# A first stage that takes its input by halves, turns it between the products, and builds its sines later

## The chip, the cores and the metric

The kernel runs on one core of a Trainium2 chip. A core has a matrix engine (TensorE, PE in the rows; PEld is its weight load), a vector engine (VectorE, DVE), a scalar engine (ScalarE, ACT), a general engine (GpSimd, POOL) and a queue engine (SyncE, SP), all with their own instruction streams, which meet at semaphores; transfers run on 16 DMA engines and are issued from the SP and ACT streams. The metric is the device time of one execution in microseconds, the median of several.

## The reference

Two layers of a block (an input projection, a pooling branch, a latent attention with rotary positions, a gated merge) and then a second block (differential attention, a recurrent branch, a mixture of experts) over 16 meta tokens and 512 tokens of width 1024. What matters here is the very beginning of layer 0:

```python
meta = jnp.broadcast_to(meta_tokens[None].astype(x.dtype), (B, N_META, D_MODEL))
h_res = jnp.concatenate([meta, x], axis=1)
...
h = rmsnorm(h_res, norm_gain[l])
proj = h @ w_in[l]
u_pool, z_pool, c_q, c_kv, k_rope, z_mla, g_pool, g_mla = jnp.split(proj, IN_SPLIT_POINTS, axis=-1)
```

and, inside the attention, `apply_rope`, which needs the cosine and sine of position times frequency.

## The kernel before

Activations are kept transposed: `hres` holds 8 chunks of 128 features by T = 528 tokens. The input arrives as rows of tokens (`xin`, 4 x 128 tokens by 1024 features), so TensorE turns it: chunk c is four 128x128 transposes into one PSUM accumulator, and a copy (VectorE, or ScalarE for c = 2, 5, 7) puts it into `hres`.

Products are done in fp32 precision from two parts. An "upper" part is a rounded copy (`h_upper`, `weights_upper`, on ScalarE: the gain is multiplied in there), a "lower" part is what the rounding lost (`h_lower`, `weights_lower`, on VectorE in this stage), and each product is upper x upper, upper x lower and lower x upper: 3 matmuls for each of 8 chunks and each of 2 halves of the tokens, 48 matmuls of 128x264 for 128 output features. The products of the projection come in the order c0 to c7 (the latents), u0 to u3 (the pooling input), rope. c0 and c1 are done together, chunk by chunk, by `first_products`, so that they can begin when chunk 0 is there; the others by `product_split`. Weights come by SP in granules of 256 columns: cq0 serves c0 and c1, cq1 serves c2 and c3, and so on. `weights_upper(c + 3)` stands behind the emptying of product c on ScalarE, since there are three places for upper weights.

The norm is applied late: `squares` on ScalarE fills 8 tiles, POOL adds them up, the product `ss_h` with a matrix of ones sums over the partitions, ScalarE takes the root (`root`, a Sqrt), VectorE the reciprocal (`inverse`), and the u products are scaled with it when they are emptied.

Before all this, VectorE works out the rotation angles from the positions (12 small instructions), and ScalarE takes the two sines. A table of gains and biases (`vrows`, `vrows2`) is turned by TensorE as well ("vecs", "vec2"), and so are the sines ("trig"); `turn_tables` on TensorE and `turned_tables` on VectorE do the last two, in layer 0 behind c2, with `ss_h` ahead of them. TensorE runs `keep_busy` matmuls (products with nothing that anyone reads) while the input arrives.

PSUM has four accumulators, taken in turn; TensorE waits for the reader of the one it takes again. All engines run in program order, which is the order of the code.

Of the kernel before, what the change touches and what calls it, by code (L numbers as in the profile page):

```python
# [16 lines left out]
I32 = mybir.dt.int32  # L17
# [5 lines left out]
P = 128  # L23
D = 1024
# [20 lines left out]
LV = 22  # L45
# [156 lines left out]
def program(nc, a, out, known=None, debug=None):  # L202
    n = Counts(known)
    mark, at, now = n.mark, n.at, n.now
    with ExitStack() as ctx:
# [70 lines left out]
        vrows2 = qkf[:, 5 * D + P:5 * D + 2 * P]  # L276

# [30 lines left out]
        X_BY_ACT = (2, 5, 7)  # L308

# [86 lines left out]
        x_loaded = sem("x_loaded")  # L396
# [260 lines left out]
        def _(sp):  # L657
            sp.dma_start(const[:, :], a["const"][:, 0:K_TIE]).then_inc(const_loaded, 16)

            sp.dma_start(krope[NOPE:QK, 0, META:T].bitcast(I32),  # L660
                         a["positions"].to_broadcast([ROPE, SEQ])).then_inc(const_loaded, 16)

            sp.wait_ge(pool_made, at(pool_made, "vrows"))
            for l in range(LAYERS):
                r = LV * l
                for name, r0, k, m in (("norm_gain", 0, DC, P), ("q_a_norm_gain", 8, QC, P),
                                       ("kv_a_norm_gain", 14, KC, P), ("pool_scale", 16, PG, P),
                                       ("q_norm_gain", 20, 1, QK), ("k_norm_gain", 21, 1, QK)):
                    sp.dma_start(vrows[r + r0:r + r0 + k, 0:m],
# [23 lines left out]
            load_first(0, 2)  # L693
# [10 lines left out]
            load_first(2, 4)  # L704
# [110 lines left out]
        def _(pe):  # L815
# [17 lines left out]

            def done(ins, label):
                ins.then_inc(psum_filled, 1)
                mark(psum_filled, label)
# [71 lines left out]
            dst = accumulator("vecs", dve_evacuated)  # L908
            keep_busy(dst[:, 1, :], 7, work[:, 0, 0:512])
            pe.wait_ge(const_loaded, 32)  # L910
            pe.wait_ge(gains_loaded, at(gains_loaded, "gains"))
            done(nc.tensor.transpose(dst[:, 0, 0:LAYERS * LV], vrows[0:LAYERS * LV, :],
                                     ident[0:LAYERS * LV, 0:LAYERS * LV]), "vecs")
            pe.wait_ge(x_loaded, 80)
            dst = accumulator("meta", dve_evacuated)
            for c in range(DC):
# [3 lines left out]
            for c in range(DC):  # L920
                dst = accumulator(("x", c), act_evacuated if c in X_BY_ACT else dve_evacuated)
# [3 lines left out]
            def turn_tables():  # L925

                pe.wait_ge(vec_loaded, at(vec_loaded, "vec2"))
# [12 lines left out]
            for n.layer in range(LAYERS):  # L940
# [603 lines left out]
        def _(act):  # L1544
# [4 lines left out]
            for i in range(4):  # L1549
                act.dma_start(xin[:, i, :], a["x"][0, i * P:(i + 1) * P, :]).then_inc(x_loaded, 16)  # L1550
            act.dma_start(metain[0:META, :], a["meta_tokens"]).then_inc(x_loaded, 16)
            act.wait_ge(dve_made, at(dve_made, "angles"))

            nc.scalar.activation(sinT, krope[NOPE:QK, 0, :], ACT.Sin).then_inc(act_made, 1)
            mark(act_made)
            nc.scalar.activation(cosT, krope[NOPE:QK, 1, :], ACT.Sin, scale=-1.0,
                                 bias=small[NOPE:QK, 0:1]).then_inc(act_made, 1)
            mark(act_made, "trig")
# [60 lines left out]
            act.wait_ge(dve_evacuated, at(dve_evacuated, "vecs"))  # L1619
# [1631 lines left out]
```

## Time and profile before

| | us |
|---|---|
| median of 3 runs | 1812.49 |
| lowest and highest run | 1810.97, 1815.47 |
| the profiled execution's own time | 1814.62 |
| its span in the trace | 1812.7 |
| TensorE busy | 1751.2 (97%) |
| VectorE busy | 1181.4 (65%) |
| ScalarE busy | 876.7 (48%) |
| GpSimd busy | 342.9 (19%) |
| mean granted TensorE clock | 0.987 of full |

The span is the time from the first to the last instruction in the trace; the execution's own time has 1.9 us around it. TensorE is busy in nearly the whole span, so what counts is where it waits or where its clock is low. A clock of 0.50 in a row is 1.2 GHz, 1.00 is 2.4 GHz.

### The profile page before, as it was taken

How to read it: one execution, taken by the hardware profiler on the slowest of the kernel's cores; microseconds unless marked ns; L12 is line 12 of the kernel's file. 1: busy time of each engine (PE TensorE's matmuls, PEld its weight loads, DVE VectorE, ACT ScalarE, POOL GpSimd, SP SyncE). 2: the span in 40 equal slices, each digit the busy share in tenths (PEclk: the TensorE clock that was granted, in tenths of full speed). 3: DMA queues.
4: the chain of work that ended last, by engine and by line, in shares of the span. 5: the costliest groups of instructions: out<-in, count | busy, mean ns of one | idle time of the engine just before them, and what ended most of it. 6: DMA issues, size and time to landing. Idle time of an engine off the chain costs nothing.

```text
span 1812.7 us, 25327 instructions
## 1 busy us (share of the span) xinstructions
PE 1751.2 (97%) x10148; PEld 1440.3 (79%) x10148; DVE 1181.4 (65%) x1700; ACT 876.7 (48%) x1411; POOL 342.9 (19%) x228
## 2 busy tenths in 40 slices
PE   8999999999999999999999999999999999999993
PEld 6998788999898677788999776765568868888882
DVE  5575644554456655555776598586774566889896
ACT  5425434334334544334344365556552356777771
POOL 3323222001242322001000276310010120000001
PEclk8999999999999999999999999999999989999997
DMA  6203111323311212323222110213243449999994
GB/s 190 77 24 99 48 48 54 110 71 116 96 60 59 66 45 71 101 93 98 94 93 77 64 48 24 69 48 95 68 151 117 143 172 375 403 404 403 403 376 174
DMA packets 156095, 241.31 MB, mean 133 GB/s; under 512 B 9593, under 2 KB 101018, under 8 KB 155978
## 3 DMA queue, kind: packets, MB, share of 16 engines
q1 hardware_dynamic: 148602, 212.88, 34.2%
q0 software_dynamic: 4464, 16.25, 2.4%
q10 hardware_dynamic: 2912, 10.55, 1.5%
q8 instruction: 82, 1.34, 0.3%
q14 instruction: 35, 0.29, 0.1%
HBM read 223.41 MB, written 16.25 MB: 132 GB/s over the span
## 4 chain that ended last, share of the span: by engine, by line
PE 51%; DVE 5%; ACT 4%; issue 1%; DMA 1%; POOL 0%; POOLq 0%; ACTq 0%; DVEq 0%
PE acc L1408 15%; PE acc L879 10%; PE acc L1123 9%; PE acc L1148 7%; PE acc L1212 2%; PE acc L1226 2%; PE acc L1243 1%; PE acc L1392 1%; PE acc L1234 1%; PE acc L1108 1%; DVE upad L2749 1%; DVE qk L2749 1%; ACT v L2007 1%; DMA qk<-y_rows,back_rows 0%; PE acc L1030 0%
## 5 line engine op out<-in xcount | busy, mean ns | idle before, releaser
L879 PE MATMUL acc<-h_split,ring_split 128*128 128x264 f32 (+1 forms) x864 | 269.4, 312 | 0.0
L879 PEld LDWEIGHTS acc<-h_split,ring_split 128*128 128x128 f32 x864 | 162.3, 188 | 9.7
L1148 PE MATMUL acc<-ring_split,h_split 128*128 128x256 f32 x384 | 107.9, 281 | 0.0
L879 PE MATMUL acc<-h_split,qk_split 128*128 128x264 f32 (+1 forms) x288 | 92.6, 322 | 1.3 <-DVE ring_split L2253 1.3
L879 PE MATMUL acc<-ring_split,qk_split 128*128 128x264 f32 (+1 forms) x288 | 92.2, 320 | 0.0
L2253 DVE TENSOR_TENSOR ring_split<-ring,o_split 128x1024 fp32r<-128x1024 f32 (+1 forms) x32 | 44.9, 1418 | 64.3 <-ACT o_split L1569 64.1
L3065 POOL TENSOR_TENSOR latent<-latent 128x528 f32<-128x528 f32 x18 | 26.8, 1490 | 292.9 <-ACT latent L1564 292.5
L2253 DVE TENSOR_TENSOR ring_split<-ring,qk_split 128x1024 fp32r<-128x1024 f32 (+1 forms) x56 | 59.4, 1070 | 34.0 <-ACT qk_split L1569 34.0
L879 PE MATMUL acc<-h_split,krope_split 128*128 128x264 f32 (+1 forms) x240 | 79.4, 331 | 1.9 <-POOL ring_split L3079 1.9
L879 PE MATMUL acc<-ring_split,krope_split 128*128 128x264 f32 (+1 forms) x240 | 77.0, 321 | 0.0
L3079 POOL TENSOR_TENSOR ring_split<-ring,krope_split 128x1024 fp32r<-128x1024 f32 x20 | 48.1, 2406 | 152.5 <-ACT krope_split L1569 152.5
L1123 PE MATMUL acc<-h_split,ring_split 128*128 128x512 f32 x192 | 75.6, 394 | 0.0
L1148 PEld LDWEIGHTS acc<-ring_split,h_split 128*128 128x128 f32 x384 | 72.3, 188 | 0.0
L1569 ACT ACTIVATE qk_split<-ring 128x1024 fp32r<-128x1024 f32 (+2 forms) x60 | 57.4, 965 | 23.4 <-PE acc L879 22.6
L2500 DVE TENSOR_SCALAR latent<-latent,small 128x144 f32<-128x144 f32 (+4 forms) x72 | 66.2, 919 | 2.6
L879 PE MATMUL acc<-work_split,qk_split 128*128 128x264 f32 (+1 forms) x192 | 61.6, 321 | 0.0
L879 PE MATMUL acc<-upad_split,ring_split 128*128 128x264 f32 (+1 forms) x192 | 61.6, 321 | 0.0
L879 PE MATMUL acc<-h_split,o_split 128*128 128x264 f32 (+2 forms) x208 | 61.4, 295 | 0.0
L879 PE MATMUL acc<-ring_split,o_split 128*128 128x264 f32 (+2 forms) x208 | 60.7, 292 | 0.0
L3197 POOL DMA_INDIRECT latent<-h_rows,rows_of x16 | 15.1, 943 | 237.3 <-PE acc L1392 219.6
L879 PEld LDWEIGHTS acc<-h_split,qk_split 128*128 128x128 f32 x288 | 54.1, 188 | 5.7 <-issue 1.7
L879 PEld LDWEIGHTS acc<-ring_split,qk_split 128*128 128x128 f32 x288 | 54.2, 188 | 4.1
(599 smaller groups left out, 5571.8 us busy)
## 6 DMA issues: line engine op xcount, KB each, us to landing
ring<-in_w_in SPq DMA_DIRECT2D x64, 1024.0 KB, 5.2
ring<-in_w_expert_gate SPq DMA_DIRECT2D x10, 2048.0 KB, 12.7
ring<-in_w_expert_up SPq DMA_DIRECT2D x10, 2048.0 KB, 12.0
ring<-in_w_expert_down SPq DMA_DIRECT2D x10, 2048.0 KB, 13.2
ring<-in_w_out SPq DMA_DIRECT2D x12, 1024.0 KB, 5.2
y_rows<-gate ACTq DMA_DIRECT2D x16, 512.0 KB, 6.9
hres<-in_w_expert_up SPq DMA_DIRECT2D x3, 2048.0 KB, 11.6
qk<-in_w_expert_down SPq DMA_DIRECT2D x3, 2048.0 KB, 14.4
```

The costliest lines, as they stand in the source:

```text
L879: ins = nc.tensor.matmul(dst[0:rows_, half, 0:x.shape[1]], w[:, k, :], x, start=(k == 0 and i == 0), stop=(k == last and i == 2), skip_gro ...
L1123: ins = nc.tensor.matmul(dst[:, 0, :], w[:, k, :], x, start=(k == 0 and i == 0), stop=(k == DC - 1 and i == 2), skip_group_check=True)
L1148: ins = nc.tensor.matmul(dst[:, side, 0:WIDE], x[k][:, rows_], w, start=(k == 0 and part == 0), stop=(k == DC - 1 and part == 2), skip_gro ...
L1212: ins = nc.tensor.matmul(lx_at[-1], w[:, k, :], moved[k], start=x == 0, stop=x == LX_PASSES - 1, skip_group_check=True)
L1226: ins = nc.tensor.matmul(dst[:, c, :], q2[r, hd, i * P:(i + 1) * P], k2[r, hd, :], start=True, stop=True)
L1408: ins = nc.tensor.matmul(dst, x, w, start=start and i == 0, stop=stop and i == 2, skip_group_check=True)
L1569: nc.scalar.activation(dst, src, ACT.Copy).then_inc(act_made, 1)
L2253: made(nc.vector.tensor_tensor(dst, src, up.bitcast(F32), ALU.subtract), label)
L2500: made(ts(probs[s % 3][0:nt, 0:t0 + nt], probs[s % 3][0:nt, 0:t0 + nt], r, None, ALU.mult), ("p", s))
L2749: made(nc.vector.tensor_tensor_scan(m_[:, back_], a_[:, back_], x_[:, back_], 0.0, ALU.mult, ALU.add), ("scan", u))
L3065: ins = nc.gpsimd.tensor_tensor(latent[:, 0, :] if c < DC - 1 else sum_sq, latent[:, 0, :], latent[:, c, :], ALU.add)
L3079: nc.gpsimd.tensor_tensor(dst, src, up.bitcast(F32), ALU.subtract).then_inc(pool_made, 1)
```

## The change

All of it is in the first stage of layer 0. The input comes in two halves of the features instead of four quarters of the tokens, in turn with the weights: cq0 from SP beside half 0 from ACT, cq1 only once half 1 has landed. The identity matrix and the first gain come by their own small transfers; the other constants, the positions and the gains come behind. Chunks 0 to 3 are turned ahead of the products (with short `keep_busy` matmuls between them), chunks 4 to 7 behind the products of k = 0 to 3, in the accumulators that chunks 2 to 5 had. On ScalarE each chunk's square stands behind its upper part, not behind all of them. The angles are worked out on VectorE between the lower weights of c3 to c7, the sines follow the emptying of c6, and `ss_h`, the tables and what reads them stand behind c7 in layer 0.

```diff
+        SUMS_AT = (7, 2)
+        ANGLES_AT = 6
...
-            load_first(0, 2)
+            load_first(0, 1)
+            sp.wait_ge(x_loaded[1], 16)
+            load_first(1, 2)
+            sp.dma_start(angles[:, 0, META:T].bitcast(I32),
+                         a["positions"].to_broadcast([ROPE, SEQ])).then_inc(const_loaded, 16)
+            sp.dma_start(const[:, P:], a["const"][:, P:K_TIE]).then_inc(const_loaded, 16)
+            load_first(2, 4)
...
+                    if n.layer == 0 and k < 4:
+                        n.layer = None
+                        turn_input(k + 4)
+                        n.layer = 0
...
-            keep_busy(dst[:, 1, :], 7, work[:, 0, 0:512])
+            keep_busy(dst[:, 1, :], 3, work[:, 0, 0:512])
...
+            def turn_input(c):
+
+                if c % 4 == 0:
+                    pe.wait_ge(x_loaded[c // 4], 16)
+                by = act_evacuated if c in X_BY_ACT else dve_evacuated
+                if c < 4:
+                    dst = accumulator(("x", c), by)
+                else:
+                    dst = accumulator_again(("x", c), by, 4 - c % 2)
                 for i in range(4):
                     ins = nc.tensor.transpose(dst[:, 0, i * P:(i + 1) * P], xin[:, i, c * P:(c + 1) * P], ident)
                 done(ins, ("x", c))
+
+            for c in range(4):
+                turn_input(c)
+                keep_busy(acc[:, 3, 1, 0:256], 1 if c < 2 else 0, work[:, 0, 0:256])
+            keep_busy(acc[:, 3, 1, :], 3, work[:, 0, 0:512])
...
                     product_split(("c", c), act_evacuated, h_up, h_low)
-                    if c == 2:
-                        product("ss_h", act_evacuated, [ones[:, :]], lambda k: sum_sq,
-                                before=lambda k: pe.wait_ge(square_sum, at(square_sum, "sum", back=1)))
+                    if c == SUMS_AT[n.layer]:
                         if n.layer == 0:
                             n.layer = None
                             turn_tables()
                             n.layer = 0
+                        product("ss_h", act_evacuated, [ones[:, :]], lambda k: sum_sq,
+                                before=lambda k: pe.wait_ge(square_sum, at(square_sum, "sum", back=1)))
...
+            input_upper(0)
+            input_copy(2)
+            input_upper(1)
+            first_upper(0)
+            first_upper(1)
+            for c in range(2):
+                squares(c, ("x", c), ("sq0", c))
+            for c in range(2, 4):
+                input_upper(c)
+                squares(c, ("x", c), ("sq0", c))
...
-                    if c == 2:
+                    if n.layer == 0 and c == ANGLES_AT:
+                        n.layer = None
+                        rotation_tables()
+                        n.layer = 0
+                    if c == SUMS_AT[n.layer]:
                         root("ss_h", inv[:, :], D, 1)
...
-                for i in range(3 if n.layer == 0 else 2, 6):
-                    weights_lower(JOBS_A, i)
-                inverse("ss_h", inv[:, :])
                 if n.layer == 0:
+                    for i in range(3, DC):
+                        weights_lower(JOBS_A, i)
+                        if i < 7:
+                            n.layer = None
+                            (angles_begun, angles_turns, angles_reduced, angles_ended)[i - 3]()
+                            n.layer = 0
                     n.layer = None
                     turned_tables()
                     n.layer = 0
-                for i in range(6, DC):
-                    weights_lower(JOBS_A, i)
+                    layer_vectors()
+                    inverse("ss_h", inv[:, :])
```

How the instructions stand now: first TensorE at the start of the program, up to the first product (`const,qk` are transposes of the input, `work,ones` is `keep_busy`, L895 and L915 are the first products). Before:

```order
L841 MATMUL acc<-work,ones 128x512 x6
L912 MATMUL acc<-const,qk 128x44 [waits gains_loaded,const_loaded]
L917 MATMUL acc<-const,qk 128x16 [waits x_loaded]
L917 MATMUL acc<-const,qk 128x16 x7
L923 MATMUL acc<-const,qk 128x128 x8
...
L895 MATMUL acc<-h_split,o_split 128x264 [waits dve_made,act_evacuated,dve_evacuated,pool_made]
```

and of the change:

```order
L940 MATMUL acc<-const,qk 128x16 [waits meta_loaded]
L940 MATMUL acc<-const,qk 128x16 x7
L954 MATMUL acc<-const,qk 128x128 [waits x_loaded0]
L954 MATMUL acc<-const,qk 128x128 x3
L861 MATMUL acc<-work,ones 128x256
L954 MATMUL acc<-const,qk 128x128 x4
L861 MATMUL acc<-work,ones 128x256
L954 MATMUL acc<-const,qk 128x128 [waits dve_evacuated]
...
L861 MATMUL acc<-work,ones 128x512 x3
L915 MATMUL acc<-h_split,o_split 128x264 [waits dve_made,dve_evacuated,pool_made]
```

Four chunks instead of eight stand ahead of the first product, and `keep_busy` has moved from ahead of the input to between and behind its chunks.

Then VectorE in layer 0, from the lower part of c7's weights to that of u2's (L2253 and L2344 are `weights_lower`; the one from `zp_split` behind the reciprocal of `inv` is u0's). Before, u0's stands behind c7's, both behind the reciprocal:

```order
L2324 RECIPROCAL inv<-inv 128x528 [waits act_evacuated]
L2288 COPY vec<-acc 128x121 [waits psum_filled,dve_step]
L2292 COPY trig<-acc 128x160 [waits psum_filled]
...
L2253 TENSOR_TENSOR ring_split<-ring,o_split 128x8x128 [waits act_made] x2
L2349 TENSOR_TENSOR trig<-trig,rope_gain 128x160 [waits rest_loaded]
L2350 TENSOR_TENSOR trig<-trig,rope_gain 128x160
L2253 TENSOR_TENSOR ring_split<-ring,zp_split 128x8x128 [waits act_made]
```

and of the change:

```order
L2344 TENSOR_TENSOR ring_split<-ring,o_split 128x8x128 [waits act_made]
L2402 COPY vecs<-acc 128x36 [waits psum_filled]
L2405 COPY vec<-acc 128x121 [waits psum_filled]
...
L2446 RECIPROCAL inv<-inv 128x528 [waits act_evacuated,dve_step]
L2480 TENSOR_TENSOR trig<-trig,rope_gain 128x160 [waits rest_loaded,dve_step]
L2481 TENSOR_TENSOR trig<-trig,rope_gain 128x160
L2344 TENSOR_TENSOR ring_split<-ring,zp_split 128x8x128 [waits act_made]
```

The reciprocal, which waits for ScalarE's root of `ss_h`, has moved from ahead of the lower weights of c6 and c7 to behind them, and u0's lower weights still stand behind it.

And TensorE between c7 and u0. Before, u0 (L879) follows c7 directly; of the change:

```order
L899 MATMUL acc<-h_split,ring_split 128x264
L967 MATMUL acc<-const,qk 128x44 [waits act_evacuated,gains_loaded,const_loaded]
L971 MATMUL acc<-const,qk 128x121 [waits act_evacuated,vec_loaded]
L977 MATMUL acc<-const,trig 16x32 [waits act_evacuated,act_made]
...
L880 MATMUL acc<-gate,ones 128x264 [waits square_sum,act_evacuated]
L880 MATMUL acc<-gate,ones 128x264
L899 MATMUL acc<-h_split,zp_split 128x264 [waits dve_made,dve_evacuated]
```

The tables and `ss_h` (L880) now stand between c7 and u0, and u0 is the next thing behind them.

## Rows read from the trace of the kernel before

**Rows 1.** A stretch of the head: length, busy time (and instructions) of each engine, clock, DMA.

```profile
20.00:22.00 2.00, 0.00 (x0) 0.00 (x0) 1.70 (x3) 1.99 (x3) 0.00 (x0) 0.50 1.10 344
```

**Rows 2.** Timeline of TensorE in the head: start, length, line, operation, count.

```profile
1.54 9.25 PE L841 MATMUL acc<-work,ones 128*128 128x512 f32 x14 [1.54 <-DVE work L2219]
...
6.79 0.33 PEld L841 LDWEIGHTS acc<-work,ones 128*128 128x128 f32 x1 [0.52 <-issue]
7.63 0.19 PEld L841 LDWEIGHTS acc<-work,ones 128*128 128x128 f32 x1 [0.50 <-issue]
...
11.58 2.84 PE L923 MATMUL acc<-const,qk 128*128 128x128 f32 x24
18.57 1.12 PE L923 MATMUL acc<-const,qk 128*128 128x128 f32 x4 [0.97 <-DVE hres L2275]
22.20 0.56 PE L895 MATMUL acc<-h_split,o_split 128*128 128x264 f32 x1 [2.51 <-DVE ring_split L2265]
...
28.20 0.28 PE L895 MATMUL acc<-h_split,o_split 128*128 128x264 f32 x1
```

**Rows 3.** DMA: GB/s in 40 slices of 1 us; the last quarter of the input.

```profile
GB/s 0 38 206 421 377 362 399 408 399 182 337 349 345 350 350 332 309 238 385 350 348 341 324 168 93 53 54 8 2 0 0 0 0 0 0 0 0 28 163 388
...
qk<-in_x ACTq DMA_DIRECT2D x1, 512.0 KB, 7.7
```

**Rows 4.** Groups by form, 0 to 26 us: busy us, mean ns, idle before.

```profile
L2265 DVE SCALAR_TENSOR_TENSOR ring_split<-hres,vecs,h_split 128x528 fp32r<-128x528 f32 x8 | 6.1, 765 | 1.3 <-ACT h_split L1616 1.3
L1616 ACT ACTIVATE h_split<-hres,vecs 128x528 fp32r<-128x528 f32 x8 | 5.9, 734 | 2.4 <-DVE hres L2275 2.3
...
L2275 DVE COPY hres<-acc 128x512 f32<-128x512 f32 x5 | 3.3, 686 | 0.3 <-PE acc L923 0.3
...
L2253 DVE TENSOR_TENSOR ring_split<-ring,o_split 128x1024 fp32r<-128x1024 f32 x2 | 2.4, 1224 | 0.1
...
L1569 ACT ACTIVATE o_split<-ring 128x1024 fp32r<-128x1024 f32 x2 | 2.1, 1041 | 0.0
...
L1625 ACT ACTIVATE hres<-acc 128x512 f32<-128x512 f32 x3 | 1.7, 575 | 0.0
```

**Rows 5.** Timeline of TensorE at the starts of c2, c3 and u0.

```profile
36.55 0.28 PE L879 MATMUL acc<-h_split,zp_split 128*128 128x264 f32 x1
...
44.11 0.39 PE L879 MATMUL acc<-h_split,o_split 128*128 128x264 f32 x1
...
73.22 0.28 PE L879 MATMUL acc<-h_split,zp_split 128*128 128x264 f32 x1
```

**Rows 6.** Timeline of ScalarE: the squares, the root behind c2, the emptying of c7.

```profile
25.30 4.36 ACT L1564 ACTIVATE latent<-hres 128x528 f32<-128x528 f32 x8
...
44.65 1.28 ACT L1644 ACT_TABLE_LOAD   x1
45.94 0.70 ACT L1644 ACTIVATE inv<-acc,small 128x528 f32<-128x528 f32 x1
...
73.42 0.61 ACT L1655 ACTIVATE work<-acc 128x528 f32<-128x528 f32 x1 [3.74 <-PE acc L879]
...
74.42 1.06 ACT L1569 ACTIVATE o_split<-ring 128x1024 fp32r<-128x1024 f32 x1
```

**Rows 7.** Timeline of VectorE: the reciprocal, the gain products, u0's lower weights.

```profile
46.67 3.45 DVE L2324 RECIPROCAL inv<-inv 128x528 f32<-128x528 f32 x1 [0.45 <-ACT inv L1644]
...
59.60 0.31 DVE L2349 TENSOR_TENSOR trig<-trig,rope_gain 128x160 f32<-128x160 f32 x1
...
63.91 1.58 DVE L2253 TENSOR_TENSOR ring_split<-ring,zp_split 128x1024 fp32r<-128x1024 f32 x1 [3.76 <-ACT zp_split L1569]
```

**Rows 8.** Stretches around an idle gap later on: length, TensorE busy (instructions), clock, DMA.

```profile
576.00:577.00 1.00, 0.00 (x0) 1.00 0.00 0
577.00:578.00 1.00, 0.15 (x1) 0.81 0.00 0
...
581.00:582.00 1.00, 1.00 (x6) 0.98 0.00 0
```

More of the change, by code:

```diff
@@ L276, in program @@
         vrows2 = qkf[:, 5 * D + P:5 * D + 2 * P]
+        first_gain = qkf[:, 5 * D + 2 * P:5 * D + 3 * P]
+        angles = v[:, :, :].rearrange("p c t -> p (c t)")[NOPE:QK, 0:2 * T].rearrange("p (a t) -> p a t", a=2)
         sum_sq = gate[:, 1, :]
@@ L395, in program @@
         const_loaded = sem("const_loaded")
-        x_loaded = sem("x_loaded")
+        x_loaded = [sem(f"x_loaded{i}") for i in range(2)]
+        meta_loaded = sem("meta_loaded")
+        ident_loaded = sem("ident_loaded")
+        first_gain_loaded = sem("first_gain_loaded")
         vec_loaded = sem("vec_loaded")
@@ L657, in _, with load_gains @@
         def _(sp):
[L658 to L664, printed above, removed]
+            def load_gains(l):
                 r = LV * l
@@ L832, in accumulator, with accumulator_again @@
                 return acc[:, slot, :, :]
+            def accumulator_again(label, reader, back):
+                for x in jobs[-back]:
+                    released(*x)
+                slot = (len(jobs) - back) % ACCS
+                jobs[-back] = [(label, reader, n.layer)]
+                n.slots[label, n.layer] = slot
+                return acc[:, slot, :, :]
             def done(ins, label):
@@ L2231, in _ @@
-            big = 1.5 * 2 ** 23
-            chain(ts(turns, ang, 1.0 / (2 * math.pi), big, ALU.mult, ALU.add))
-            chain(ts(turns, turns, -big, None, ALU.add))
-            rest, parts = 2 * math.pi, []
-            for bits in (8, 12, 24):
-                e = 2.0 ** (bits - 1 - math.floor(math.log2(abs(rest))))
-                parts.append(math.trunc(rest * e) / e if bits < 24 else rest)
-                rest -= parts[-1]
-            for part in parts:
-                chain(stt(out=ang, in0=turns, scalar=-part, in1=ang, op0=ALU.mult, op1=ALU.add))
@@ L2241, in _, with angles_begun @@
-            chain(ts(krope[NOPE:QK, 0, :], ang, 3.1415925, -3.1415925, ALU.min, ALU.max))
-            dve.wait_ge(dve_step, now(dve_step))
-            made(stt(out=krope[NOPE:QK, 1, :], in0=krope[NOPE:QK, 0, :], scalar=-1.0,
-                     in1=krope[NOPE:QK, 0, :], op0=ALU.mult, op1=ALU.max), "angles")
-            result("vecs")
-            slot = n.slot(("vecs"))
-            evacuated(nc.vector.tensor_copy(vecs[:, :], acc[:, slot, 0, 0:LAYERS * LV]), "vecs")
+            def angles_begun():
+                dve.wait_ge(const_loaded, 32)
+                nc.vector.tensor_copy(ang[:, 0:META], const[NOPE:QK, K_META:K_META + META])
+                chain(nc.vector.tensor_copy(ang[:, META:T], angles[:, 0, META:T].bitcast(I32)))
+                chain(ts(ang[:, META:T], ang[:, META:T], float(META), None, ALU.add))
+                chain(ts(ang, ang, const[NOPE:QK, K_FREQ:K_FREQ + 1], None, ALU.mult))
@@ new lines, in angles_turns, with angles_reduced @@
+            def angles_turns():
+                big = 1.5 * 2 ** 23
+                chain(ts(turns, ang, 1.0 / (2 * math.pi), big, ALU.mult, ALU.add))
+                chain(ts(turns, turns, -big, None, ALU.add))
+            def angles_reduced():
+                rest, parts = 2 * math.pi, []
+                for bits in (8, 12, 24):
+                    e = 2.0 ** (bits - 1 - math.floor(math.log2(abs(rest))))
+                    parts.append(math.trunc(rest * e) / e if bits < 24 else rest)
+                    rest -= parts[-1]
+                for part in parts:
+                    chain(stt(out=ang, in0=turns, scalar=-part, in1=ang, op0=ALU.mult, op1=ALU.add))
@@ new lines, in angles_ended @@
+            def angles_ended():
+                chain(ts(angles[:, 0, :], ang, 3.1415925, -3.1415925, ALU.min, ALU.max))
+                dve.wait_ge(dve_step, now(dve_step))
+                made(stt(out=angles[:, 1, :], in0=angles[:, 0, :], scalar=-1.0,
+                         in1=angles[:, 0, :], op0=ALU.mult, op1=ALU.max), "angles")
+            result("first_gain")
+            slot = n.slot(("first_gain"))
+            evacuated(nc.vector.tensor_copy(vecs[:, 0:DC], acc[:, slot, 0, 0:DC]), "first_gain")
@@ L2332, in _ @@
                     n.layer = 0
-                for i in range(6, DC):
-                    weights_lower(JOBS_A, i)
+                    layer_vectors()
+                    inverse("ss_h", inv[:, :])
+                else:
+                    for i in range(2, 6):
+                        weights_lower(JOBS_A, i)
+                    inverse("ss_h", inv[:, :])
+                    for i in range(6, DC):
+                        weights_lower(JOBS_A, i)
                 def gain_of(x, count):
```

146 lines of the change are left out of this document (92 added, 54 removed).

## The prediction

> **What bounds the kernel now.** The page first: TensorE is busy for 97% of the 1812.7 us. So a change here is worth the time by which it moves a product of TensorE that everything behind it follows, less any wait that it adds. Then the timeline of the head [rows 2]: keep-busy matmuls from 1.54 to 10.8 us, six chunks turned in 2.84 us from 11.58, the last one at 18.57, the first product at 22.20. Between 20 and 22 us TensorE does nothing and its clock is at 0.50, 1.2 GHz [rows 1]; ScalarE and VectorE are both busy there, so the wait is for the elementwise work of chunk after chunk. Third, the starts of the later products [rows 5]: c2 at 36.55, c3 at 44.11, u0 at 73.22, so c3 to c7 take 5.82 us each without a wait, and 44.11 - 36.55 - 5.82 = 1.74 us is `ss_h` with the tables. Last, what stands around the root of `ss_h`, on ScalarE and VectorE [rows 6, 7].
>
> **The change part by part.**
>
> *Transfers.* By the slices [rows 3] 2.21 MB had moved at 9 us. Half 0 (1.05 MB), cq0 (1.05 MB) and the small pieces (0.13 MB) make 2.23 MB, so half 0 has landed at 9.1 us at the latest if the two share evenly, and at 8.5 if it gets two thirds (0.43 MB of smalls and cq0 first, then 1.05 x 1.5). I take 8.8. Before, the whole input had landed at about 9.8 us (issued near 2.1, 7.7 to landing [rows 3]). Half 1 lands at about 12.3 (3.28 MB in the same slices) and cq1 at about 17, both ahead of their use. The angles need constants and positions only at some 35 us. The gains land behind; the tables need them at some 65 us. These cost nothing under cover of c2 to c7; without it a late one would be its own delay.
>
> *The head, to the first product.* It needs chunk 0 turned, emptied and split, and, in this order on ScalarE, upper 0, the copy of chunk 2, upper 1, then the upper weights of c0 and c1; then VectorE's two lower weights. Lengths [rows 4]: copy 0.69 (VectorE) and 0.58 (ScalarE), upper part 0.73, upper weights 1.04, lower weights 1.22. A turned chunk is 2.84/6 = 0.47 us at the high clock and 1.12 at the low one [rows 2]; a keep-busy matmul of 512 columns is two passes, 0.84 apart at the low clock (6.79 to 7.63) and half that behind it, so the 256-column one is 0.85 or 0.43.
> At the high clock from 8.8: chunk 2 is turned at 8.8 + 3 x 0.47 + 2 x 0.43 = 11.1; copy 11.7, upper 1 12.4, upper weights 13.5 and 14.5, lower weights of c1 16.0 with the semaphores between. At the low clock chunk 2 is turned at 8.8 + 3 x 1.12 + 2 x 0.85 = 13.9, and the same chain ends at 18.7. Three keep-busy matmuls end at 14.1 and, if the clock has risen by then, at 17.6: hidden; if it stays low they end at 20.1 and hold the products.
> Which clock? Before, weight loads shortened at 7.63, after 6.1 us of unbroken keep-busy work [rows 2]. Now that work ends at 1.54 + 6 x 0.85 = 6.65, some small transposes follow, then TensorE waits for half 0. So the high clock at 8.8 is not sure, and may come during the chunks. I take the middle, 17.3, and keep 16.0 and 18.7 as ends (20.1 as the far one).
>
> *The products c0 and c1.* 96 matmuls at 5.82/48 = 0.121 us are 11.6, and four chunks turned between them 4 x 0.47 = 1.9: 13.5 us, so c2 starts at 30.8 instead of 36.55, 5.75 earlier (before, 14.35 for the same 96, of which 5.8 at the low clock, 22.2 to 28.0 [rows 2]). ScalarE must keep up: from its upper weights at some 16 us, eight squares (4.4 [rows 6]), six uppers (4.4), two copies (1.2), one upper weights (1.0) are 11, with waits for chunks 5 and 7 about 12.5: 28.5, against 29.4 when the last chunk's products begin. Hidden, with 1 us to spare; each us beyond would be on the path. POOL's sum ends 1.4 us behind the last square; it then holds c0's emptying for nothing, since c3's weights have 5.8 us of c2 as cover.
>
> *The sines, angles, squares.* VectorE's 12 angle instructions lie between lower weights that have two products of 5.82 us as cover; the sines end 0.9 us before c7 does: 0.2 + 2.06 behind c6's end to the end of the upper weights, then a table load of 1.28 and two sines, taken as 0.70 each like the Sqrt [rows 6]. Cost nothing; without the cover up to 1 us at the "trig" transposes.
>
> *`ss_h` behind c7: the wait it adds.* Call U the time at which c7's matmuls have been issued (73.22 before, when u0 started at once). Now c2 to c7 take 6 x 5.82 = 34.9, so U = 30.8 + 34.9 = 65.7. TensorE's own work behind it is 1.74 + 0.23 ("vecs"), to U + 1.97. Then u0 needs its lower weights, and these stand on VectorE behind the reciprocal of `ss_h`. That chain [rows 6, 7]: ScalarE empties c7 from U + 0.20 (73.42), ends its upper weights at U + 2.26 (75.48), loads the Sqrt table (1.28) and takes the root, which by the rows 44.65 to 46.64 are 1.99: U + 4.25. The reciprocal, 3.45: U + 7.73. Two gain products, 0.24 apart and 0.31 long: U + 8.32. The lower weights, 1.58 beside a working POOL: U + 9.90. u0 starts at U + 9.95, 75.65. TensorE idles 8.0 us (7.6 if the subtraction takes the 1.22 of [rows 4]). Before, this chain had c3 to c5 as cover. Behind u0, in the same queue, wait u1's and u2's lower weights, which u0's own time covers.
> The row has 1.28 us for a table load, with the Sqrt 0.01 us behind it. The Trainium skill (ScalarE: Activation LUTs, "What ACT_TABLE_LOAD costs") gives 2.66 for a switch, 1.38 of it a drain; no such drain shows here; by it the wait would be 9.4 and the sum 1.4 higher.
>
> *The clock behind the wait.* Later in this trace TensorE idled from about 575.5 to 577.9, the clock fell before 578 and was back at 581: 3.2 us at half speed, 1.6 lost [rows 8]. In the head 5.8 us at half speed lost 2.75 (14.35 against 11.6). An idle time of 8 us will bring it down; the cost is 1.6 to 2.8, and I take 2.3, nearer the head's, which runs the same stream of matmuls.
>
> **The sum.** Head -5.75; `ss_h` and tables only moved; "vecs" +0.23; wait +8.0; clock +2.3: +4.8 us. The shift should go through unchanged, since transfers and engines behind it are released by TensorE's products. The span becomes 1817.5 and the profiled execution's 1814.62 about 1819.4; the median of the runs, 1812.49, becomes 1817.3.
>
> **The rivals.** Changes within 0.3% (5.4 us) are about what this kernel's measurement can't tell from none.
> *Slower by more: the low clock in the head.* The input's chunks are turned at 1.2 GHz, the first product begins at 18.7 to 20.1, c2 at 32.2 to 33.6: the sum is +6.2 to +7.6, 1818.7 to 1820.1. It decides from a first product at about 17.9. For it: keep-busy ends at 6.65 where the clock rose only at 7.63. Against: transposes go on in that time.
> *The input lands no earlier.* If half 0 with cq0 beside it lands at 9.8, as the whole did, the head is 1.0 later: +5.8, 1818.3. Against it: only 2.23 MB must move, not the 2.4 before.
> *A fast head.* High clock from 8.8, first product at 16.0, and 1.6 for the clock behind the wait: +2.8, 1815.3.
> *Faster.* If u0 did not feel the chain behind c7, wait and clock would go and the sum be 4.8 - 8.0 - 2.3 = -5.5, 1807. The order of instructions on VectorE speaks against it: no cover stands between c7 and u0.
>
> **How the numbers follow.** Forecast, +4.8 with the clock rising among the chunks: 0.36, of which 0.08 lies over the bound. Fast head 0.20. Low clock 0.22. Late input 0.14. Faster 0.08, 0.02 of it within the bound. So within 0.3%: 0.28 + 0.20 + 0.02 = 0.50; slower: 0.08 + 0.22 + 0.14 = 0.44; faster 0.06. The forecast's own range is 1815 to 1819; with the fast head and the low clock, and the runs' spread of some 2 us on both sides, 1812.5 to 1821.5 leaves out the fast case and the far ends.
>
> **What would show it.** A first product (first-products line) near 17.3, c2 near 30.8 and u0 near 75.7; in front of u0 an idle time of 8 us put down to VectorE's lower weights; the clock at 0.5 for some us behind it; the Sqrt table load directly behind c7's upper weights. It is wrong if u0 starts within 2 us of c7's end, if ScalarE falls behind in the products of c0 and c1 (waits on VectorE's lower parts there), or if later stages take up the shift.

## The result and the profile after

| | before | after |
|---|---|---|
| median of 11 runs, us | 1812.49 | 1818.94 |
| the profiled execution's own time, us | 1814.62 | 1819.18 |
| its span, us | 1812.7 | 1817.2 |
| mean granted TensorE clock | 0.987 | 0.986 |

One of the 11 runs after took 2482.72 us, at a mean clock of 0.651; it is left out of the ratio and hardly moves the median. The ratio is 1.0032, with a 95% interval of 1.0024 to 1.004: 5.8 us slower by the ratio (6.45 by the two medians). The interval has the bound of 0.3% inside, so the change is slower, but whether by more than the bound can't be told. The time lies 1.6 us above the forecast of 1817.3, within its range.

The timeline of TensorE in the head of the changed kernel (start, length, line, operation, count; in brackets the idle time before and what ended it) answers to [rows 2, 5]; L915 is `first_products`, L899 `product_split`:

```profile
1.54 4.38 PE L861 MATMUL acc<-work,ones 128*128 128x512 f32 x6 [1.54 <-DVE work L2298]
...
9.35 1.12 PE L954 MATMUL acc<-const,qk 128*128 128x128 f32 x4 [1.61 <-DMA qk<-in_x]
...
12.82 1.92 PE L954 MATMUL acc<-const,qk 128*128 128x128 f32 x8
...
17.49 0.36 PE L915 MATMUL acc<-h_split,o_split 128*128 128x264 f32 x1
...
27.78 0.39 PE L915 MATMUL acc<-h_split,o_split 128*128 128x264 f32 x1 [0.64 <-DVE ring_split L2356]
...
32.85 0.28 PE L899 MATMUL acc<-h_split,zp_split 128*128 128x264 f32 x1
```

Half 0 is there at 9.35; the first product starts at 17.49, 4.71 earlier than before. The clock is low while the chunks are turned (a stretch with its clock; the mean is 0.55 in the microsecond before it and 0.53 in the one behind it, so it fell at about 8.1 and rose at about 14.95), and VectorE's lower weights of c0 and c1 end at 17.34 and 18.48:

```profile
9.00:14.00 5.00, 4.65 (x18) 4.08 (x19) 2.06 (x3) 0.82 (x2) 0.00 (x0) 0.50 0.62 207
...
16.12 2.36 DVE L2344 TENSOR_TENSOR ring_split<-ring,o_split 128x1024 fp32r<-128x1024 f32 x2
...
18.53 0.39 PE L915 MATMUL acc<-h_split,o_split 128*128 128x264 f32 x1
```

So the first product (c0's) could start when its own lower weights were there, and c1's first matmul came at 18.53, behind its own.

But c2 starts at 32.85, only 3.70 earlier: the two interleaved products take 15.36 us, and there is a wait on VectorE's lower parts (L2356) among them. The groups of VectorE by form, 18.9 to 31.3 us, of the changed kernel (busy us, mean ns, idle before), show why:

```profile
L2356 DVE SCALAR_TENSOR_TENSOR ring_split<-hres,vecs,h_split 128x528 fp32r<-128x528 f32 x6 | 9.1, 1558 | 0.9 <-ACT h_split L1666 0.9
```

Before, the same operation took 765 ns [rows 4]. In these 12 us GpSimd adds squares, as its timeline shows:

```profile
18.25 4.92 POOL L3196 TENSOR_TENSOR latent<-latent 128x528 f32<-128x528 f32 x3 [17.03 <-ACT latent L1614]
24.98 5.69 POOL L3196 TENSOR_TENSOR latent<-latent 128x528 f32<-128x528 f32 x3 [1.81 <-ACT latent L1614]
30.75 1.68 POOL L3196 TENSOR_TENSOR gate<-latent 128x528 f32<-128x528 f32 x1
```

Then the end of c7 and u0, on TensorE:

```profile
67.76 0.26 PE L967 MATMUL acc<-const,qk 44*128 44x44 f32 x1
...
69.03 1.16 PE L880 MATMUL acc<-gate,ones 128*128 128x264 f32 x4
78.64 0.56 PE L899 MATMUL acc<-h_split,zp_split 128*128 128x264 f32 x1 [8.45 <-DVE ring_split L2344]
...
86.59 0.61 PE L880 MATMUL acc<-work,ones 128*128 128x264 f32 x2
```

the chain that it waits for, on ScalarE, VectorE and GpSimd (answers to [rows 6, 7]):

```profile
70.08 1.28 ACT L1719 ACT_TABLE_LOAD   x1
71.37 0.70 ACT L1719 ACTIVATE inv<-acc,small 128x528 f32<-128x528 f32 x1
```

```profile
72.17 3.45 DVE L2446 RECIPROCAL inv<-inv 128x528 f32<-128x528 f32 x1 [1.00 <-ACT inv L1719]
75.66 1.46 DVE L2480 TENSOR_TENSOR trig<-trig,rope_gain 128x160 f32<-128x160 f32 x1
77.04 0.31 DVE L2481 TENSOR_TENSOR trig<-trig,rope_gain 128x160 f32<-128x160 f32 x1
77.28 1.21 DVE L2344 TENSOR_TENSOR ring_split<-ring,zp_split 128x1024 fp32r<-128x1024 f32 x1
```

```profile
73.52 3.42 POOL L3210 TENSOR_TENSOR ring_split<-ring,qk_split 128x1536 fp32r<-128x1536 f32 x1 [3.08 <-ACT qk_split L1619]
```

and the stretches behind it (length, busy time and instructions of PE, PEld, DVE, ACT and POOL, then the granted clock, DMA):

```profile
72.00:73.00 1.00, 0.00 (x0) 0.00 (x0) 0.83 (x1) 1.00 (x2) 0.00 (x0) 0.98 0.00 0
73.00:83.00 10.00, 4.37 (x20) 4.40 (x21) 7.72 (x6) 0.44 (x1) 3.42 (x1) 0.50 0.01 2
83.00:84.00 1.00, 1.00 (x9) 1.00 (x9) 0.00 (x0) 0.00 (x0) 0.00 (x0) 0.90 0.00 0
```

The chain of the prediction stands there link by link, and TensorE stands idle for 8.45 us. The clock is at 0.50, 1.2 GHz, from about 73 to 83; u0's 48 matmuls take 86.59 - 78.64 = 7.95 us instead of 5.8. The operations of the two kernels that answer to each other are 7.57 us later behind u0, and that shift stays, within 0.25 us, for some 940 us; what happens to it then is told below, where the prediction is weighed.

### The profile page after: what moved, and what is told of

Read it like the earlier page. It is cut to its first block, busy times and chain, and to the rows that moved or that the text cites. A ratio compares the mean times of both kernels' runs of the same rounds, so it can differ in the third digit from the quotient of the medians.

```text
span 1817.2 us, 25340 instructions
## 1 busy us (share of the span) xinstructions
PE 1750.8 (96%) x10151; PEld 1441.6 (79%) x10151; DVE 1186.1 (65%) x1701; ACT 878.1 (48%) x1413; POOL 344.9 (19%) x228
## 4 chain that ended last, share of the span: by engine, by line
PE 51%; DVE 5%; ACT 4%; issue 1%; DMA 1%; POOL 0%; POOLq 0%; ACTq 0%; DVEq 0%
PE acc L1450 15%; PE acc L899 10%; PE acc L1165 9%; PE acc L1190 7%; PE acc L1254 2%; PE acc L1268 2%; PE acc L1285 1%; PE acc L1276 1%; PE acc L1150 1%; PE acc L1434 1%; DVE upad L2880 1%; DVE qk L2880 1%; ACT v L2086 1%; DMA qk<-y_rows,back_rows 0%; PE acc L1072 0%
## 5 line engine op out<-in xcount | busy, mean ns | idle before, releaser
L899 PE MATMUL acc<-h_split,ring_split 128*128 128x264 f32 (+1 forms) x864 | 270.2, 313 | 0.0
L899 PEld LDWEIGHTS acc<-h_split,ring_split 128*128 128x128 f32 x864 | 163.3, 189 | 9.6
L899 PE MATMUL acc<-h_split,qk_split 128*128 128x264 f32 (+1 forms) x288 | 92.7, 322 | 1.3 <-DVE ring_split L2344 1.3
L899 PE MATMUL acc<-ring_split,qk_split 128*128 128x264 f32 (+1 forms) x288 | 92.2, 320 | 0.0
L2344 DVE TENSOR_TENSOR ring_split<-ring,qk_split 128x1024 fp32r<-128x1024 f32 (+1 forms) x56 | 59.4, 1069 | 34.1 <-ACT qk_split L1619 34.1
L899 PE MATMUL acc<-h_split,krope_split 128*128 128x264 f32 (+1 forms) x240 | 79.4, 331 | 1.9 <-POOL ring_split L3210 1.9
L899 PE MATMUL acc<-ring_split,krope_split 128*128 128x264 f32 (+1 forms) x240 | 77.0, 321 | 0.0
L2344 DVE TENSOR_TENSOR ring_split<-ring,o_split 128x1024 fp32r<-128x1024 f32 (+1 forms) x32 | 43.8, 1391 | 45.0 <-ACT o_split L1619 44.8
L899 PE MATMUL acc<-upad_split,ring_split 128*128 128x264 f32 (+1 forms) x192 | 61.7, 321 | 0.0
L899 PE MATMUL acc<-work_split,qk_split 128*128 128x264 f32 (+1 forms) x192 | 61.6, 321 | 0.0
L899 PE MATMUL acc<-h_split,o_split 128*128 128x264 f32 (+2 forms) x208 | 61.3, 295 | 0.0
L3328 POOL DMA_INDIRECT latent<-h_rows,rows_of x16 | 16.5, 1031 | 235.0 <-PE acc L1434 217.1
L899 PE MATMUL acc<-ring_split,o_split 128*128 128x264 f32 (+2 forms) x208 | 60.7, 292 | 0.0
L899 PEld LDWEIGHTS acc<-h_split,qk_split 128*128 128x128 f32 x288 | 54.2, 188 | 5.7 <-issue 1.7
L899 PEld LDWEIGHTS acc<-ring_split,qk_split 128*128 128x128 f32 x288 | 54.2, 188 | 4.1
```

The lines of the kernel that those rows point to most:

```text
L899: ins = nc.tensor.matmul(dst[0:rows_, half, 0:x.shape[1]], w[:, k, :], x, start=(k == 0 and i == 0), stop=(k == last and i == 2), skip_gro ...
L2344: made(nc.vector.tensor_tensor(dst, src, up.bitcast(F32), ALU.subtract), label)
```

## The experiments

Each kernel was timed in five rounds beside the kernel before on the same chip, and each ratio is to that one (its medians there were 1811.57 to 1814.43), so two experiments are compared by their ratios. A shift is that of matching instructions of VectorE and ScalarE between two traces.

**u0's lower weights ahead of the chain** (with u1's; called the first version below). The changed kernel with

```diff
-                    for i in range(3, DC):
+                    for i in range(3, DC + 2):
...
-                for i in range(DC, DC + 3):
+                for i in range(DC + 2 if n.layer == 0 else DC, DC + 3):
```

> The change with one thing moved: VectorE makes the lower weights of u0 and u1 ahead of the tables and of the reciprocal, not behind them. Theory (u0 waits for its lower weights, which stand behind the reciprocal of ss_h; 8.45 us of idle TensorE and 2.15 us of low clock behind it): the wait goes, u0 starts within 0.3 us of ss_h's end, at about 70.4 us, and its products run at the high clock. The time falls by 10.6, less up to 1.5 for VectorE, which is later at the emptying of u0: about 1809 to 1811 us, 2 to 3 us under the kernel before. Rival (the chain behind c7 is only one of several equal limits, VectorE's work from u0's emptying to the units being the next): the wait comes back in front of the units and the time stays within 3 us of the change, 1816 to 1819.

1808.65 us, ratio 0.9969 (0.9957 to 0.9981). TensorE's timeline there:

```profile
68.94 1.16 PE L880 MATMUL acc<-gate,ones 128*128 128x264 f32 x4
69.74 0.48 PE L899 MATMUL acc<-h_split,zp_split 128*128 128x264 f32 x1
```

u0 follows `ss_h` at once, where it began at 78.64, and from about 120 us on everything is 10.85 us earlier than in the changed kernel. So the chain is the wait, and wait and clock together cost 10.85; without them the change would gain: there this version is 3.25 us ahead of the kernel before.

**The late sums alone.** The kernel before, with nothing but `ss_h`, the tables and their readers moved behind c7 in layer 0:

```diff
-                    if c == 2:
-                        product("ss_h", act_evacuated, [ones[:, :]], lambda k: sum_sq,
...
+                    if c == (7, 2)[n.layer]:
...
-                for i in range(3 if n.layer == 0 else 2, 6):
+                for i in range(3, DC) if n.layer == 0 else range(2, 6):
...
-                inverse("ss_h", inv[:, :])
...
+                inverse("ss_h", inv[:, :])
+                for i in range(DC if n.layer == 0 else 6, DC):
```

> The kernel before with one part of the change alone: ss_h and the tables behind c7 in layer 0, with VectorE's reciprocal behind the lower weights of c7. The head is that of before. Theory: u0 waits 8 to 8.5 us and runs its first 4 us at the low clock, 2.2 us lost; 10.5 us over the kernel before, about 1823. Rival (the loss is the new head's, or comes from accumulators taken in another turn): no more than 2 us over before, about 1814.

1822.02 us, ratio 1.0049 (1.0036 to 1.0062). One row of TensorE says it:

```profile
81.57 0.56 PE L879 MATMUL acc<-h_split,zp_split 128*128 128x264 f32 x1 [8.83 <-DVE ring_split L2253]
```

The shift to the kernel before is 9.85 us behind u0. The same wait arises with the old head, so it belongs to the place of the sums and not to the input.

**TensorE kept busy in the wait.** The changed kernel, in two sizes:

```diff
+                        if n.layer == 0:
+                            keep_busy(acc[:, 2, 1, :], 18, const[:, 0:512])
```

> The change with 18 keep-busy matmuls of 512 columns between ss_h and u0 (7.7 us at the high clock; nobody reads them). Theory (the low clock behind the wait costs 2.15 us by itself): u0 starts when it did, or up to 0.5 us later, and runs all its matmuls 0.12 apart; 1.5 to 2.2 us less than the change, 1816.7 to 1817.5. Rival (the clock there costs nothing, since VectorE sets the pace of the next stretch): the same as the change, within 0.5 us.

18 were too many: with two passes each they took 15.61 us, held u0 to about 85.9, and all behind it came 4.99 us later than in the changed kernel. So 1822.76 us, ratio 1.0052 (1.0039 to 1.0065), missed the expectation and says nothing of the clock's price. With 9 in place of 18:

> The changed kernel with nine keep-busy matmuls between the reduction of the sum and u0: 18 passes of 0.43 us are 7.8 us, from about 70.3 to 78.2, so that they end before u0's weights are there (u0 began at 78.64 with a wait of 8.45 us). Theory (the low granted clock behind the wait costs u0 and its neighbours 2.15 us): u0 begins at about 78.7 at a granted clock of 1.00, its 27 matmuls take 5.8 instead of 7.95 us, and the kernel gains 1.5 to 2.2 us on the changed one, about 1816.8 to 1817.5 us. Rival (the clock behind the wait is not what makes them slow, or it is taken back later): no difference from the changed kernel, 1818.9.

1816.16 us, ratio 1.002 (1.0011 to 1.0029). The passes end before u0's weights are there, and the clock stays up (the timeline of TensorE, and a stretch with its clock):

```profile
69.29 7.89 PE L861 MATMUL acc<-const,ones 128*128 128x512 f32 x18
77.92 0.36 PE L899 MATMUL acc<-h_split,zp_split 128*128 128x264 f32 x1 [0.74 <-DVE ring_split L2346]
```

```profile
78.00:84.00 6.00, 6.00 (x49) 5.98 (x50) 2.06 (x3) 0.00 (x0) 0.00 (x0) 1.00 0.01 3
```

Ahead of the wait this execution ran 0.70 us earlier than the changed kernel's, behind u0 2.80: the clock's price is 2.10 us. In the times alone this is not clear: the intervals of this ratio and the changed kernel's overlap.

**The squares behind all upper parts**, as before the change, in the changed kernel:

```diff
-            for c in range(2):
-                squares(c, ("x", c), ("sq0", c))
...
-                squares(c, ("x", c), ("sq0", c))
...
-            squares(4, ("x", 4), ("sq0", 4))
...
-            squares(5, ("x", 5), ("sq0", 5))
...
+            for c in range(DC):
```

> The change with the squares as before, behind all upper parts on ScalarE, so that GpSimd's sum hardly runs beside VectorE's lower parts. Theory (the lower parts took 1.8 us instead of 0.77 because GpSimd was adding squares at the same time, and this, not ScalarE, stretched the products of c0 and c1 from 13.5 to 15.4 us): lower parts back at 0.77 us until the sum starts, c2 starts at 30.9 to 31.6 instead of 32.85. The sum ends some 3 us later and holds the emptying of c0, so c3's weights may be 1 to 2 us late: the time within 1.5 us of the change. Rival (the lower parts are slow for another reason, such as the accumulators read beside them or the transfers): they stay at 1.8 us and c2 at 32.8.

1822.96 us, ratio 1.0051 (1.0037 to 1.0066). VectorE's groups by form in the same stretch as above, and ScalarE's first emptying:

```profile
L2352 DVE SCALAR_TENSOR_TENSOR ring_split<-hres,vecs,h_split 128x528 fp32r<-128x528 f32 x6 | 4.5, 764 | 2.7 <-ACT h_split L1666 2.7
```

```profile
38.15 0.61 ACT L1726 ACTIVATE work<-acc 128x528 f32<-128x528 f32 x1 [6.77 <-POOL gate L3192]
```

and the start of c3 on TensorE, with the clock behind it:

```profile
41.61 0.56 PE L899 MATMUL acc<-h_split,o_split 128*128 128x264 f32 x1 [4.70 <-DVE ring_split L2340]
...
40.00:47.00 7.00, 5.39 (x24) 5.42 (x25) 6.63 (x6) 4.10 (x7) 5.41 (x4) 0.51 0.01 2
```

The lower parts are back at 764 ns, and from the first product (17.06) to c2 (30.93) it is 13.87 us: the 13.5 of the prediction, nearly. But GpSimd's sum now ends at 38.05, c0's accumulator is emptied into tiles that the sum reads, and the emptying waits 6.77 us for it (32.52 in the changed kernel, 38.15 here). c3's weights come behind that. TensorE waits 4.70 us for them and starts c3 2.94 later than the changed kernel (41.61, not 38.67); the low clock behind the wait makes it 5.44 by the end of the stage. The time missed the expectation, which was within 1.5 us of the change. The prediction's view that the sum "holds c0's emptying for nothing" is right for the changed order only.

**The squares behind, into tiles of their own**, on top of the first version, so that c0's emptying in layer 0 needs no sum:

```diff
+        first_squares = ([upad[:, g, PAD:] for g in range(PG)] + [zp[:, g, :] for g in range(2)]
+                         + [gate[:, 0, :], krope[:, 0, :]])
...
-                    if c == 0:
+                    if c == 0 and n.layer:
```

> The first version with u0's and u1's lower weights ahead of the tables, and the squares of stage one behind all upper parts, into tiles of their own, so that the emptying of c0's accumulator does not wait for GpSimd's sum. Theory (VectorE's lower parts take 1.5 to 1.8 us instead of 0.77 because GpSimd adds squares beside them, which costs the products of c0 and c1 1.9 us; the late sum cost 5.6 us only because c0's emptying waited for it): c2 begins at about 31 instead of 32.85, c0 is emptied without a wait, and the kernel gains about 1.9 us, 1806.7. Rival (GpSimd's additions move behind and slow VectorE's gate and evictions of c1 to c3 by as much): 1808.5 or more.

1806.88 us, ratio 0.9964 (0.995 to 0.9978). c2 starts at 31.02 instead of 32.78, and c0 is emptied at 31.38 without a wait; c0 and c1 take 13.87 us again. The shift to the first version is 1.74 us in the stage and 1.93 at 1000 us, near the 1.9 expected; 0.28 of it stands already at the first product, which comes at 17.15. By the two ratios the gain is 0.9, and their intervals overlap.

**Five keep-busy matmuls at the start** of the changed kernel, instead of three:

```diff
-            keep_busy(dst[:, 1, :], 3, work[:, 0, 0:512])
+            keep_busy(dst[:, 1, :], 5, work[:, 0, 0:512])
```

> The changed kernel with five instead of three keep-busy matmuls at the start (4 more passes of 0.73 us, ending at about 8.8 instead of 5.9 us, half 0 landing at 9.3). Theory (the head after the landing is bound by TensorE at the low clock: transposes of 1.06 us and more where the granted clock is 0.50): the clock is at 1.00 when the transposes begin or soon after, the first product begins at about 16.3 instead of 17.49, and the kernel gains about 1.2 us, 1817.7. Rival (the head is bound by the landing and by the evictions, not by TensorE's clock): first product at 17.3 to 17.5, no difference.

1817.34 us, ratio 1.0025 (1.0016 to 1.0034). TensorE and the clock there:

```profile
1.54 6.47 PE L861 MATMUL acc<-work,ones 128*128 128x512 f32 x10 [1.54 <-DVE work L2298]
...
9.32 0.66 PE L954 MATMUL acc<-const,qk 128*128 128x128 f32 x4 [0.65 <-DMA qk<-in_x]
...
15.32 0.36 PE L915 MATMUL acc<-h_split,o_split 128*128 128x264 f32 x1 [0.59 <-DVE ring_split L2344]
```

```profile
9.00:12.00 3.00, 2.68 (x21) 2.48 (x22) 1.64 (x3) 0.98 (x2) 0.00 (x0) 1.00 0.76 296
```

In the changed kernel, too, the last two keep-busy passes start only 0.43 apart, at the high clock; but they end at 5.92, and the clock is down again from about 8.1, ahead of half 0. Here the work ends at 8.01, the clock is still at 1.00 when half 0 lands, and a turned chunk takes 0.66 instead of 1.12. In all seven programs with three keep-busy matmuls the clock fell before half 0 landed or within 0.3 us of it (8.1 to 9.7), in none of the three with five. The first product starts 2.17 us earlier, and the shift of 2.16 stays through the first stage. The gain in the median is smaller (some 1.3 us by the two ratios) and its interval overlaps with the changed kernel's.

**This with the first version**, and then with the squares' own tiles as well:

> The first version with u0's and u1's lower weights ahead of the tables, and five keep-busy matmuls at the start. Theory: both gains add, 1808.7 less 1.2, about 1807.5 us. Rival: the earlier first product is lost again in the wait for VectorE's lower parts of the first two chunks, since those do not come earlier: 1808.5.

1806.17 us, ratio 0.9964 (0.9952 to 0.9977). The first product starts at 15.58 instead of 17.43 and c2 at 30.94 instead of 32.78: nothing is lost between them.

> The three edits together: u0's and u1's lower weights ahead of the tables, five keep-busy matmuls at the start, and the squares of stage one behind all upper parts in tiles of their own. Theory (the earlier first product and the undisturbed lower parts of c0 and c1 are separate gains): first product at about 15.4, c2 at about 29.5, some 1.3 us less than with either alone, 1804.9. Rival (c2 is held by VectorE's lower parts whichever comes first, so that the earlier first product is lost behind them): 1806.2 to 1806.9, as with one of them.

1804.83 us, ratio 0.9958 (0.9945 to 0.9971): first product at 15.38, c2 at 29.28. The gains add. By the two ratios this is some 13.4 us under the changed kernel, and it is faster than the kernel before by 0.42%, or 7.6 us, of which some 2.4 come from a place at 1031 us that is told in the next section.

**The gain products ahead of the reciprocal**, in the changed kernel:

```diff
                     layer_vectors()
-                    inverse("ss_h", inv[:, :])
...
                      "gained")
+                if n.layer == 0:
+                    inverse("ss_h", inv[:, :])
```

> The changed kernel with the two gain products ahead of the reciprocal on VectorE, where it idles 1.00 us for the root. Their 0.55 us and the 1.15 us by which the first was prolonged (1.46 instead of 0.31 us) then lie ahead of the chain. Theory (a VectorE operation that reads two tiles waits for a GpSimd operation that began earlier; the first gain product waited for GpSimd's subtraction of 73.52 to 76.94): u0's lower weights, which come next, meet the same subtraction and are prolonged to its end, so that u0 begins only some 0.3 us earlier, 1818.6 us. Rival (the prolonged gain product was its own, of its operands or first use): the lower weights begin at 75.7 and take 1.21, u0 begins 1.65 us earlier, 1817.3.

1818.77 us, ratio 1.0027 (1.0018 to 1.0036). VectorE and GpSimd there:

```profile
71.18 0.32 DVE L2479 TENSOR_TENSOR trig<-trig,rope_gain 128x160 f32<-128x160 f32 x1
71.42 0.32 DVE L2480 TENSOR_TENSOR trig<-trig,rope_gain 128x160 f32<-128x160 f32 x1
72.08 3.45 DVE L2446 RECIPROCAL inv<-inv 128x528 f32<-128x528 f32 x1 [0.34 <-ACT inv L1719]
75.56 2.43 DVE L2344 TENSOR_TENSOR ring_split<-ring,zp_split 128x1024 fp32r<-128x1024 f32 x1
```

```profile
73.49 3.42 POOL L3211 TENSOR_TENSOR ring_split<-ring,qk_split 128x1536 fp32r<-128x1536 f32 x1 [3.09 <-ACT qk_split L1619]
```

The gain product is 0.32 where GpSimd is idle. Now u0's lower weights, 1.21 before, take 2.43: they begin in GpSimd's operation and end 1.08 us behind its end at 76.91. The time has only changed its owner; TensorE's wait goes from 8.45 to 8.0. So the prolonged operation is not special: here the one that comes next on VectorE and reads two tiles pays. The reciprocal, which reads one, took 3.45 beside GpSimd in both.

## Why the prediction came out as it did

The sum behind u0 was +4.8 and is +7.57; u0 starts at 78.64 and not 75.65. By parts, measured: head -3.70 (-5.75 forecast), "vecs" +0.23, wait +8.8 (8.0), clock +2.15 (2.3), which make +7.5. The path is the one of the prediction; the head and the wait were mis-sized, by 2.05 and 0.8. That the time came out only 1.6 us above the forecast is luck: some 2.4 us that nobody forecast were won far behind (see "To the median").

*Transfers.* Half 0 is there at 9.35, 8.8 were forecast, and no later transfer is waited for. But the way to the 8.8 was wrong: in [rows 3] the first eight slices of 1 us add up to 2.21 MB, so that much had moved at 8 us and not at 9, and the same working would have given about 7.8.

*First product.* 17.3 forecast, 17.49 measured, and this is luck as well. The clock did not rise among the chunks, as the middle value had it. All four were turned at 0.50, and the low case is what came: chunk 2 turned at 13.9 (half 0 came later, and chunks took 0.85 to 0.91 and not 1.12) and c1's lower weights done at 18.48, against 13.9 and 18.7. But the prediction let the first product wait for c1's lower weights, and it needs c0's alone, which are done 1.14 earlier. The run of five keep-busy matmuls shows the fast end (15.32 for the first product, and 16.32 for the end of c1's lower weights; forecast 16.0).

*The products c0 and c1.* This is the term that was mis-sized most: 13.5 forecast, 15.36 measured. ScalarE kept up, as was worked out; VectorE was not looked at. "These cost nothing" for the moved squares missed that GpSimd's additions now lie beside VectorE's lower parts, 1558 ns instead of 765. The squares behind the upper parts give 13.87, so GpSimd's part is 1.49 of the 1.86. The effect stood in the prediction's own rows: it priced u0's lower weights at 1.58 "beside a working POOL", and no other operation so.

*The wait.* The chain is right in each link, its length is not: moving u0 ahead of it took 78.64 - 69.74 - 0.07 (the later c2) = 8.83 us off u0's start, 8.0 were forecast. The first gain product took 1.46 where 0.31 was taken from [rows 7], and the lower weights 1.21 where 1.58 was taken: +1.15 - 0.37 = +0.78. Idle time in the rows is 8.45, since the modelled end of the matmuls of `ss_h` lies 0.4 us behind the place where u0 could follow. The table load is 1.28 with the root 0.01 behind it, as in [rows 6]. The further 1.38 of the Trainium skill (ScalarE: Activation LUTs, "What ACT_TABLE_LOAD costs") does not show here either.

*The clock behind the wait.* 2.3 forecast, 2.15 in the rows, 2.10 when it was kept up.

*"Faster".* This rival was that u0 does not feel the chain, 1807. It does; the version in which it cannot came out at 1808.65. Its -5.5 is not confirmed by that: the first version is 3.25 us ahead of the kernel before up to 1020 us, since its head is no better, and the rest comes from the place that follows.

*To the median.* "The shift should go through unchanged" failed. It falls from 7.36 to 4.98 between 1031 and 1058 us, where no instruction was changed. There GpSimd's subtraction and a VectorE operation that reads two tiles start almost together. Before (GpSimd, VectorE, then what TensorE waits for):

```profile
1026.90 2.36 POOL L3150 TENSOR_TENSOR ring_split<-ring,o_split 128x1024 fp32r<-128x1024 f32 x1 [152.07 <-ACT o_split L1569]
1026.91 2.90 DVE L2701 SCALAR_TENSOR_TENSOR gate<-gate,rt 128x512 f32<-128x512 f32 x1
...
1029.86 0.66 PE L1234 MATMUL acc<-const,gate 128*128 128x128 f32 x4 [1.96 <-DVE gate L2701]
```

and in the changed kernel:

```profile
1034.14 0.75 DVE L2832 SCALAR_TENSOR_TENSOR gate<-gate,rt 128x512 f32<-128x512 f32 x1
1034.26 2.84 POOL L3281 TENSOR_TENSOR ring_split<-ring,o_split 128x1024 fp32r<-128x1024 f32 x1 [152.05 <-ACT o_split L1619]
```

Before, GpSimd is first by 0.01 us, and VectorE takes 2.90 us; now VectorE is first by 0.12, takes 0.75, and TensorE's wait of 1.96 is gone. This is no chance of one execution: GpSimd is first in both traces of the old head (with the late sums by 0.04, and TensorE waits 1.94), VectorE by 0.12 to 0.13 in all ten of the new. Why the new head moves the two by that little was not tried.

A second step, 0.85 at 1495 to 1507, is the clock. The length of a stretch at 0.50 differs there from execution to execution. Here is a part of it, first of the changed kernel, then of the one with the gain products ahead, at the same place in the program; before, the mean is 0.50 in 1488 to 1492, which answers to 1493 to 1497:

```profile
1493.00:1496.00 3.00, 2.59 (x6) 1.25 (x7) 0.74 (x1) 3.00 (x3) 0.00 (x0) 1.00 0.74 240
...
1493.00:1496.00 3.00, 2.60 (x3) 1.17 (x4) 0.75 (x1) 3.00 (x3) 0.00 (x0) 0.50 0.55 204
```

Behind it the second is 0.6 us later, though it had no shift up to there. What sets the length was not tried. Between the two profiled executions 4.56 is left at the end, between the medians 6.45 and by the ratio 5.8, with an interval of some 4.4 to 7.2 us.

## What to carry to other kernels

When work is moved behind a product, follow the next product's weights through every queue: here three small steps on two engines had been free under c3 to c5 and cost 11 us under nothing, and two lower weights moved ahead of them gave it all back. When GpSimd work is moved, look at what VectorE does beside it and at who waits for it: an earlier sum slowed the products of c0 and c1 by 1.5 us, a later one held an accumulator for 5.6, and only tiles of its own freed both. A small shift can also turn the order in which two engines start, far behind the change (2.4 us here): look there before a gain is put down to the edit. Give TensorE something to do up to the moment at which its data arrive, and no longer: by the traces, five keep-busy matmuls gained 2.2 us in the head, nine in the wait 2.1, and eighteen lost 5.

## What the runs showed of the hardware

In these traces VectorE operations that read two tiles of SBUF do not run beside GpSimd's additions and subtractions, they alternate with them. The three lower parts of 25.88 to 31.24 us took 1.79 us each (0.76 alone) while GpSimd's three additions of 24.98 to 30.67 took 1.90 each (1.39 alone, 8.36 us for six with the squares behind). The Trainium skill (SBUF — State Buffer, "Who interferes with whom") states that a VectorE instruction with two SBUF inputs contends with a GpSimd instruction that reads SBUF, and that the shared ports are an exclusive lock. The traces agree: the first gain product ends 0.18 us behind GpSimd's subtraction (77.12 against 76.94), u0's lower weights in the last experiment 1.08 behind it, and the reciprocal, which reads one tile, is untouched at 3.45. That rule, set against the order of the squares, would have pointed at the 1.49 us that the squares cost, and at the gain product.

To read one tile only is not enough to be spared: in the changed kernel a TENSOR_SCALAR of 128x2 that began at 1036.06 took 1.07 us and ended with GpSimd's subtraction (1037.10), where the same line took 0.17 at 1043.93; at 1040.40 it took 0.55, again to the end of a GpSimd operation (1040.91).

In the same head the clock rose at different times in different executions. Five programs have the same first 17 us. In four of them it rose at about 14.9 to 15.3, with first products at 17.49, 17.43, 17.47 and 17.78 us (half 0 came 0.3 later in the last); in the fifth it was up at about 12.3 (0.94 on average in 12 to 15 us, where the changed kernel had 0.51), with the first product at 16.79. In the three programs with five keep-busy matmuls it was up ahead of the landing (first products at 15.32, 15.58 and 15.38).
